# One block per layer for output projection, norm and feed-forward, and paged values loaded page by page

## The chip, the cores and the metric

The kernel runs on one core of one Trainium2 chip. A core has five engines that run their own instruction streams and meet through semaphores: TensorE (PE; its weight loads are listed as PEld), VectorE (DVE), ScalarE (ACT), GpSimd (POOL) and SyncE (SP, which here only issues DMAs). The metric is the device time of one execution in microseconds; less is better.

## The reference

One inference step of a two-layer decoder over T = 560 tokens: a prompt of 512 tokens behind 16 meta tokens, and 8 sequences with 4 new tokens each. Model width 1024, feed-forward width 2816, all in float32.

```python
for layer in range(2):
    xn = rmsnorm(h, norm_g[layer, 0])
    mix = mixer_even(...) if layer == 0 else mixer_odd(...)   # ends in "@ w_out"
    h = h + rmsnorm(mix, norm_g[layer, 1])
    ff = swiglu(rmsnorm(h, norm_g[layer, 2]), wg, wu, wd)     # (silu(x@wg) * (x@wu)) @ wd
    h = h + rmsnorm(ff, norm_g[layer, 3])
# in mixer_even, for the 8 sequences: attention over 1024 cached positions each
gather = lambda c: c[page_table].reshape((B, past) + c.shape[2:])     # 8 pages of 128 positions
hf = fox_attend(q, F, tq, concat(gather(cache_k), k), concat(gather(cache_v), v), F, tk)
```

## The kernel before

Activations lie with features on the 128 partitions and the 560 tokens along the columns, in two column halves of 280 (`HALF`), since a PSUM bank holds 512 floats. A matrix product keeps float32 accuracy by splitting each operand into a high part (rounded to the type fp32r) and a low part (the rest); three products per pair are summed: high*high, high*low, low*high. The weights come through `ring`, two slots in SBUF that SP fills by DMA. From a slot ScalarE makes `w_high` by a cast (L241) and VectorE `w_low` by a subtraction (L245), for one tile of 128 output features at a time, and TensorE works on the other of two such pieces meanwhile. One tile with 1024 inputs is 48 matmuls of 280 columns (8 input chunks, 3 products, 2 halves).

`project` is this loop as a block of its own: four semaphores tell when a piece is split, a tile finished and a bank free. `close_layer` ends a layer. In its first block it splits the mixer's output `xn` into `mixed_high` (ScalarE, L1779) and `mixed_low` (VectorE and GpSimd, L1786) and the first weights. Then follow three calls of `project` and one of `norm`: the output projection (8 tiles), the norms, gate and up (44 tiles in 11 turns of 4), down (8 tiles of 22 input chunks, each in two pieces of 66 matmuls). In gate and up, VectorE scales the gate by the norm's factor, ScalarE takes its silu, VectorE multiplies by up, and GpSimd scales again and splits the result into `hidden_high` and `hidden_low`.

`norm` squares the projection's output, sums the squares over the partitions by matmuls with a matrix of ones (L504), takes the root on ScalarE, and then walks over the 8 chunks at full width (560 columns): VectorE scales (L584) and adds to `h` (L588), ScalarE makes the next input's high part and its squares (L540, L541), VectorE the low part (L592, after all 8 chunks). TensorE sums the second squares; `warm` gives it idle matmuls in between. The root of the second norm is taken at the start of the next `project`, where VectorE then inverts it (L408). Every `with nc.Block()` ends in a barrier of all engines.

Attention over the cache (the block from L1530 on) takes the 8 sequences in two groups of 4. Step s of 16 works on one key page of each sequence of a group: `turned` transposes four pages on TensorE, `scores` follows one step behind. SP loads keys into two sets of four slots (`load_k`: four page numbers are read into registers, then four DMAs of 256 KB) and values into four buffers of eight pages (`load_v`: eight page numbers, eight DMAs). Three of the four value buffers of the first group are filled in the block before; the second group's can be filled only when `values(0)` (step 11) has used the first group's:

```python
load_v(sp, 2)
for s in range(2, STEPS):            # STEPS = 16
    load_k(sp, s)
    if s >= STEPS - 4:
        if s == STEPS - 4:
            sp.wait_ge(v_used, 1)
        load_v(sp, 4 + s - (STEPS - 4))
```

One of the value buffers lies in `ring`, so layer 0's output weights are sent only in the first block of `close_layer`; layer 1's are already there.

## Time and profile before

| | |
|---|---|
| median of 3 runs | 1977.45 us (1973.34 to 1980.96) |
| the profiled execution's own time | 1978.11 us |
| its span, first to last instruction | 1976.6 us |
| mean granted TensorE clock | 0.921 |
| TensorE busy | 1748.8 us (88%) |
| VectorE busy | 826.0 us (42%) |
| ScalarE busy | 488.9 us (25%) |
| GpSimd busy | 297.2 us (15%) |

The profile is of one execution; the times of a row are microseconds from the start of its span. A granted clock of 1.00 is TensorE at 2.4 GHz, 0.50 is 1.2 GHz. "Idle before" in a row is the time in which the engine had nothing to do ahead of the instruction, and behind the arrow stands what ended it; PEq is TensorE's sequencer, which as a releaser here stands for a barrier at the start or end of a block.

### The profile page before, as it was taken

Reading aid. Unit: us, or ns where it says so; the run is one execution under the profiler, and the core shown is the slowest. Engines: PE = TensorE matmul, PEld = TensorE weight load, DVE = VectorE, ACT = ScalarE, POOL = GpSimd, SP = SyncE. Lnnn points to the kernel's source line nnn. Section 1 sums busy time; section 2 is a strip of 40 time slices with the busy share of each in tenths; the row PEclk is TensorE's granted clock in tenths of the full one; section 3 lists DMA queues with packets and bytes.
Section 4 is the critical chain, followed back from the end, with each engine's and each line's share of the span. In section 5 each row is a group of like instructions: output and inputs, shape, how many; then the busy total and the mean of one; then the engine's idle time right before and its main releaser. Section 6 shows DMA issues by size and latency. Waiting matters only on the chain. (4 is left out here: it accounts for less than half of the span.)

```text
span 1976.6 us, 31237 instructions
## 1 busy us (share of the span) xinstructions
PE 1748.8 (88%) x12539; PEld 1577.6 (80%) x12539; DVE 826.0 (42%) x1427; ACT 488.9 (25%) x634; POOL 297.2 (15%) x290
## 2 busy tenths in 40 slices
PE   5999897696758899999899899978488999998995
PEld 5999854555438699999899699955286999998995
DVE  3323645524333744444222633267637444442225
ACT  3111310141111433332111311133214333321111
POOL 1411001001000033333200000031300333332000
PEclk9999987597879999999899999988689999999998
DMA  4232210155652133333222122220121333332321
GB/s 124 90 91 70 65 26 0 48 171 170 219 185 77 33 85 85 85 85 93 77 79 70 42 68 85 96 68 0 50 65 43 84 85 84 85 88 73 82 56 45
DMA packets 225241, 159.60 MB, mean 81 GB/s; under 512 B 18041, under 2 KB 206437, under 8 KB 225048
## 3 DMA queue, kind: packets, MB, share of 16 engines
q1 hardware_dynamic: 220832, 156.40, 27.1%
q0 software_dynamic: 3280, 1.85, 0.4%
q8 instruction: 38, 0.62, 0.1%
q10 hardware_dynamic: 1064, 0.51, 0.1%
q14 instruction: 27, 0.22, 0.0%
HBM read 149.11 MB, written 9.88 MB: 80 GB/s over the span
## 5 line engine op out<-in xcount | busy, mean ns | idle before, releaser
L241 ACT CAST w_high<-ring 128x1024 fp32r<-128x1024 f32 (+1 forms) x188 | 207.1, 1104 | 914.1 <-PE psum L334 911.4
L334 PE MATMUL psum<-mixed_high,w_high 128*128 128x280 f32 x1664 | 352.0, 293 | 35.3 <-PEq L1770 29.0
L245 DVE TENSOR_TENSOR w_low<-ring,w_high 128x1024 fp32r<-128x1024 f32 (+1 forms) x188 | 289.6, 1544 | 155.7 <-ACT w_high L241 153.4
L334 PE MATMUL psum<-mixed_high,w_low 128*128 128x280 f32 x1664 | 353.9, 294 | 0.0
L334 PE MATMUL psum<-mixed_low,w_high 128*128 128x280 f32 x1664 | 350.9, 293 | 0.0
L334 PEld LDWEIGHTS psum<-mixed_high,w_high 128*128 128x128 f32 x1664 | 267.4, 190 | 36.9 <-issue 36.9
L334 PEld LDWEIGHTS psum<-mixed_high,w_low 128*128 128x128 f32 x1664 | 267.9, 191 | 0.0
L334 PEld LDWEIGHTS psum<-mixed_low,w_high 128*128 128x128 f32 x1664 | 265.3, 190 | 0.0
L334 PE MATMUL psum<-normed_high,w_high 128*128 128x280 f32 x832 | 175.3, 292 | 3.8 <-PEq L517 3.8
L334 PE MATMUL psum<-normed_high,w_low 128*128 128x280 f32 x832 | 175.7, 292 | 0.0
L334 PE MATMUL psum<-normed_low,w_high 128*128 128x280 f32 x832 | 174.7, 292 | 0.0
L334 PE MATMUL psum<-hidden_high,w_high 128*128 128x280 f32 x704 | 149.3, 294 | 15.7 <-PEq L298 15.7
L334 PE MATMUL psum<-hidden_low,w_high 128*128 128x280 f32 x704 | 149.5, 294 | 0.0
L334 PE MATMUL psum<-hidden_high,w_low 128*128 128x280 f32 x704 | 149.2, 294 | 0.0
L334 PEld LDWEIGHTS psum<-normed_high,w_high 128*128 128x128 f32 x832 | 132.7, 189 | 4.7 <-issue 4.7
L334 PEld LDWEIGHTS psum<-normed_high,w_low 128*128 128x128 f32 x832 | 133.1, 190 | 0.0
L334 PEld LDWEIGHTS psum<-normed_low,w_high 128*128 128x128 f32 x832 | 132.0, 189 | 0.0
L334 PEld LDWEIGHTS psum<-hidden_high,w_high 128*128 128x128 f32 x704 | 113.0, 191 | 16.1 <-issue 16.1
L432 POOL TENSOR_TENSOR silu<-silu,rstd 128x560 f32<-128x560 f32 x44 | 63.6, 1446 | 409.4 <-DVE silu L385 409.4
L395 DVE TENSOR_TENSOR projected<-psum,rstd 128x280 f32 (+1 forms) x104 | 41.9, 444 | 194.3 <-PE psum L334 194.2
L334 PEld LDWEIGHTS psum<-hidden_high,w_low 128*128 128x128 f32 x704 | 112.9, 191 | 0.0
L334 PEld LDWEIGHTS psum<-hidden_low,w_high 128*128 128x128 f32 x704 | 112.5, 190 | 0.0
(350 smaller groups left out, 1983.7 us busy)
## 6 DMA issues: line engine op xcount, KB each, us to landing
ring<-in_ffn_wg SPq DMA_DIRECT2D x44, 512.0 KB, 4.0
ring<-in_ffn_wu SPq DMA_DIRECT2D x44, 512.0 KB, 5.2
ring<-in_ffn_wd SPq DMA_DIRECT2D x16, 1408.0 KB, 6.9
projected<-in_cache_fox_k SPq DMA_DIRECT2D x64, 256.0 KB, 4.1
ring<-in_w_in_even SPq DMA_DIRECT2D x14, 1024.0 KB, 5.5
ring<-in_w_in_odd SPq DMA_DIRECT2D x12, 1024.0 KB, 5.1
v_pages<-in_cache_fox_v SPq DMA_DIRECT2D x32, 256.0 KB, 4.3
projected<-in_cache_fox_v SPq DMA_DIRECT2D x16, 256.0 KB, 4.0
```

Of the source, the lines that this page charges most:

```text
L241: nc.scalar.copy(part(high, p), raw(slot, p)).then_inc(high_done[p], 1)
L245: nc.vector.tensor_tensor(part(low, p), raw(slot, p), part(high, p).bitcast(F32), ALU.subtract).then_inc(low_done[p], 1)
L334: last = nc.tensor.matmul(banks[2 * tl + half][:, 0:HALF], w[:, k, :], m[:, half * HALF:(half + 1) * HALF], start=(kk == 0 and w is w_high ...
L395: c = nc.vector.tensor_tensor(out, banks[2 * tl + half][:, 0:HALF], rstd[:, cols_], ALU.mult)
L432: nc.gpsimd.tensor_tensor(silu[:, slot, :], silu[:, slot, :], rstd[:, :], ALU.mult)
```

## The change

`close_layer` becomes one block. The first two units of gate and up weights (four tiles) get SBUF of their own (`first_w`) and are loaded and split during the output projection. The projection's tiles 0 to 5 run at full width, tiles 6 and 7 by halves: first both tiles for tokens 0 to 279, then both for tokens 280 to 559. The norms run for the first half of the tokens and then for the second; the squares are summed chunk by chunk on VectorE (`square_sum`, `h_square_sum`) and TensorE only sums the result over the partitions. As each chunk of a half comes out of the norm, TensorE multiplies it with the four first tiles (`first_products`). Gate and up go on with 10 turns, down follows without a barrier, its first piece waiting for 10 of the 11 turns of the hidden values and its second for all. The warming matmuls of this norm are gone. `hidden` is kept by halves, so GpSimd splits by halves. VectorE makes all of `mixed_low`.

For the cache, value buffer 2 of the first group is loaded two pages ahead of each of the key steps 2 to 5, and the second group's values by page number, one page of four sequences at a time (`load_v_step`), alternating with key steps 13 to 15, the rest behind them. `values(1)` waits for each page by itself.

The semaphores of three stages (the prompt's attention, the cache's, and each `close_layer`) are cleared and given back, with a barrier behind.

```diff
+    def stage_semaphores():
+        used = []
+        def new(name):
+            sems[name] = sems.get(name, 0) + 1
+            used.append(nc.alloc_semaphore(name=f"{name}_{sems[name]}"))
+            return used[-1]
+        def close():
+            nc.clear_and_free_semaphores(used)
+            nc.all_engine_barrier()
+        return new, close
...
+    def load_v_step(sp, pg):
+        _, pages = nc.values_load_multi_w_load_instructions(
+            step_ids[0:1, bass.ds(4 * (PAGES + pg), 4)], engines=[mybir.EngineType.SP], min_val=0, max_val=NPHYS - 1)
+        for slot, page in enumerate(pages):
+            sp.dma_start(vpage[slot][:, pg * 512:(pg + 1) * 512],
+                         cache_v[bass.ds(page, 1), :, :].rearrange("a t n -> (a t) n")).then_inc(v_step[pg], 16)
...
-            load_v(sp, 2)
             for s in range(2, STEPS):
+                if s < 6:
+                    load_v(sp, 2, 2 * (s - 2), 2)
                 load_k(sp, s)
-                if s >= STEPS - 4:
-                    if s == STEPS - 4:
-                        sp.wait_ge(v_used, 1)
-                    load_v(sp, 4 + s - (STEPS - 4))
+                if s == STEPS - 3:
+                    sp.wait_ge(v_used, 1)
+                if s >= STEPS - 3:
+                    load_v_step(sp, s - (STEPS - 3))
+            for pg in range(3, PAGES):
+                load_v_step(sp, pg)
...
+                for n in (6, 7):
+                    pe.wait_ge(w_lo[n % 2], 4)
+                    half_tile(n, 0).then_inc(half_done, 1)
+                pe.wait_ge(o_acc, 5)
+                mm(banks[1][:, 0:HALF], ones[:, :], acc[:, HALVES[0]], start=True, stop=False)
+                pe.wait_ge(o_sq, 13)
+                mm(banks[1][:, 0:HALF], ones[:, :], sq[6][:, HALVES[0]], start=False, stop=False)
+                half_tile(6, 1).then_inc(used[0], 1)
+                pe.wait_ge(o_sq, 14)
+                mm(banks[1][:, 0:HALF], ones[:, :], sq[7][:, HALVES[0]], start=False, stop=True).then_inc(o_sum, 1)
+                half_tile(7, 1).then_inc(used[1], 1)
...
+                def first_products(k, a, tiles):
+                    pe.wait_ge(xh_done, KC * a + k + 1)
+                    for t in tiles:
+                        bank = banks[2 * t + a][:, 0:HALF]
+                        if k == 0 and a == 0:
+                            pe.wait_ge(first_lo, t + 1)
+                        mm(bank, fw[t][0][:, k], x_h[:, k, HALVES[a]], start=(k == 0), stop=False)
+                        mm(bank, fw[t][1][:, k], x_h[:, k, HALVES[a]], start=False, stop=False)
+                    pe.wait_ge(xl_done, KC * a + k + 1)
+                    for t in tiles:
+                        last = mm(banks[2 * t + a][:, 0:HALF], fw[t][0][:, k], x_l[:, k, HALVES[a]], start=False,
+                                  stop=(k == KC - 1))
...
+                pe.wait_ge(h_acc, 2 * KC - 2)
+                pe.wait_ge(h_root, 1)
+                mm(banks[7][:, 0:HALF], ones[:, :], acc_h[:, HALVES[1]], start=True, stop=True).then_inc(h_sum, 1)
+                pe.wait_ge(h_root, 2)
+                for k in range(KC):
+                    first_products(k, 1, (3,))
...
+                            for s in range(2):
+                                pe.wait_ge(hid_done[s], 10 + p)
...
+                for a in range(2):
+                    c = HALVES[a]
+                    dve.wait_ge(o_root, a + 1)
+                    v.reciprocal(rpost[:, c], rpost[:, c])
...
+                    for step in range(KC + 3):
+                        k = step
+                        if k < KC:
+                            v.scalar_tensor_tensor(out=o[:, k, c], in0=o[:, k, c], scalar=gain(layer, 1, k), in1=rpost[:, c],
+                                                   op0=ALU.mult, op1=ALU.mult).then_inc(y_done, 1)
+                        k = step - 1
+                        if 0 <= k < KC:
+                            dve.wait_ge(y_done, KC * a + k + 1)
+                            v.tensor_tensor(h[:, k, c], h[:, k, c], o[:, k, c], ALU.add).then_inc(h_done, 1)
+                        k = step - 2
+                        if 0 <= k < KC:
+                            dve.wait_ge(xh_done, KC * a + k + 1)
+                            v.scalar_tensor_tensor(out=x_l[:, k, c], in0=h[:, k, c], scalar=gain(layer, 2, k),
+                                                   in1=x_h[:, k, c].bitcast(F32), op0=ALU.mult,
+                                                   op1=ALU.subtract).then_inc(xl_done, 1)
+                        k = step - 3
+                        if 1 <= k < KC:
+                            dve.wait_ge(h_sq, KC * a + k + 1)
...
+                            v.tensor_tensor(acc_h[:, c], sq[0][:, c] if k == 1 else acc_h[:, c], sq[k][:, c],
+                                            ALU.add).then_inc(h_acc, 1)
...
+                up_low(0, 0, 5)
+                for a in range(2):
+                    dve.wait_ge(h_root, a + 1)
+                    v.reciprocal(rstd[:, HALVES[a]], rstd[:, HALVES[a]])
```

Three places show the new order. On SP, at the start of the cache block, before (L1287 are values, L1281 keys; an ISA row prepares a register):

```order
L1287 ISA
L1287 DMA v_pages<-in_cache_fox_v 128x512
L1287 ISA
L1287 DMA v_pages<-in_cache_fox_v 128x512
L1275 TENSOR_LOAD step_ids
L1275 ISA x8
L1281 ISA
L1281 DMA projected<-in_cache_fox_k 128x512
L1281 ISA
L1281 DMA projected<-in_cache_fox_k 128x512
```

and SP at the same place now (L1305 are values, L1297 keys):

```order
L1302 TENSOR_LOAD page_ids
L1302 ISA x4
L1305 ISA
L1305 DMA v_pages<-in_cache_fox_v 128x512
L1305 ISA
L1305 DMA v_pages<-in_cache_fox_v 128x512
L1291 TENSOR_LOAD step_ids
L1291 ISA x8
L1297 ISA
L1297 DMA projected<-in_cache_fox_k 128x512
```

Two value pages now stand ahead of the first keys of this block; before there were eight, of which the rows show the last two.

On PE, between output projection and gate and up of a layer, before (L298, L543, L517 and L312 are branches into and out of blocks):

```order
L334 MATMUL psum<-mixed_high,w_low 128x280 x2
L316 REGISTER_ALU
L316 COMPARE_AND_BRANCH
L298 UNCONDITIONAL_BRANCH
L543 UNCONDITIONAL_BRANCH
L451 MATMUL psum<-ones 128x512 x4
L504 MATMUL psum<-squares,ones 128x280 x8
L451 MATMUL psum<-ones 128x512 x8
L504 MATMUL psum<-squares,ones 128x280 x16
L517 UNCONDITIONAL_BRANCH
```

and PE there now (L1889 ends the last half tile of the projection, L1937 to L1941 are `first_products`):

```order
L1889 MATMUL psum<-mixed_high_6555,w_low_6554 128x280
L1937 MATMUL psum<-mixed_high_6555,first_w_high_6561 128x280
L1938 MATMUL psum<-mixed_high_6555,first_w_low_6562 128x280
L1937 MATMUL psum<-mixed_high_6555,first_w_high_6561 128x280
L1938 MATMUL psum<-mixed_high_6555,first_w_low_6562 128x280
L1937 MATMUL psum<-mixed_high_6555,first_w_high_6561 128x280
L1938 MATMUL psum<-mixed_high_6555,first_w_low_6562 128x280
L1937 MATMUL psum<-mixed_high_6555,first_w_high_6561 128x280
L1938 MATMUL psum<-mixed_high_6555,first_w_low_6562 128x280
L1941 MATMUL psum<-mixed_low_6556,first_w_high_6561 128x280 x4
```

The sums and warming matmuls between the two products are gone from this place, and the second product starts chunk by chunk.

On DVE, in the norm, before (two rows of the scaling and adding loop, then all low parts):

```order
L584 SCALAR_TENSOR_TENSOR squares<-projected_out,cols,rstd 128x560
L588 TENSOR_TENSOR h<-h,squares 128x560 x2
L592 SCALAR_TENSOR_TENSOR mixed_low<-h,cols,mixed_high 128x560 x8
L517 UNCONDITIONAL_BRANCH
L369 UNCONDITIONAL_BRANCH
L408 RECIPROCAL rstd<-rstd 128x280 x2
```

and DVE in the norm now, one step of the first half:

```order
L2142 SCALAR_TENSOR_TENSOR projected_out_6548<-projected_out_6548,cols,post_rstd_6559 128x280
L2147 TENSOR_TENSOR h<-h,projected_out_6548 128x280
L2151 SCALAR_TENSOR_TENSOR mixed_low_6556<-h,cols,mixed_high_6555 128x280
L2159 TENSOR_TENSOR h_square_sum_6572<-squares_6563,squares_6564 128x280
```

The low part of a chunk now comes in the same step as its neighbours' scaling, at half the width, and a sum of squares has come to VectorE.

## Rows read from the trace of the kernel before

**Rows 1.** Windows: busy us by engine in stretches (us from the span's start)

```profile
core 0: us, PE busy (x) PEld busy (x) DVE busy (x) ACT busy (x) POOL busy (x), PEclk, DMA share, GB/s
525.00:563.00 38.00, 19.36 (x188) 16.25 (x190) 9.82 (x19) 4.68 (x8) 0.00 (x0) 0.65 0.83 271
649.30:679.80 30.50, 24.30 (x73) 12.91 (x73) 29.34 (x36) 17.53 (x27) 2.69 (x2) 1.00 0.00 1
706.00:953.20 247.20, 247.19 (x1923) 246.97 (x1921) 100.74 (x119) 77.71 (x78) 83.02 (x60) 1.00 0.33 88
953.20:961.00 7.80, 0.00 (x0) 0.00 (x0) 5.04 (x4) 1.36 (x1) 5.81 (x3) 0.70 0.00 1
961.00:966.60 5.60, 5.57 (x24) 5.57 (x25) 0.00 (x0) 0.00 (x0) 0.00 (x0) 0.50 0.88 243
```

**Rows 2.** Timeline, VectorE, norm of layer 0: start, us, line, operation

```profile
636.92 0.81 DVE L398 COPY projected_out<-psum 128x280 f32<-128x280 f32 x2 [3.81 <-PE psum L334]
649.27 0.81 DVE L398 COPY projected_out<-psum 128x280 f32<-128x280 f32 x2 [5.37 <-PE psum L334]
656.37 2.35 DVE L245 TENSOR_TENSOR w_low<-ring,w_high 128x1024 fp32r<-128x1024 f32 x2
663.87 0.73 DVE L588 TENSOR_TENSOR h<-h,squares 128x560 f32<-128x560 f32 x1
664.52 0.79 DVE L584 SCALAR_TENSOR_TENSOR squares<-projected_out,cols,rstd 128x560 f32<-128x560 f32 x1
673.36 5.78 DVE L592 SCALAR_TENSOR_TENSOR mixed_low<-h,cols,mixed_high 128x560 fp32r<-128x560 f32 x8
679.95 3.66 DVE L408 RECIPROCAL rstd<-rstd 128x280 f32<-128x280 f32 x2 [0.81 <-ACT rstd L357]
```

**Rows 3.** Timeline, ScalarE, layer 0, behind the projection and behind the fourth up tile

```profile
650.37 2.35 ACT L525 ACTIVATE squares<-projected_out 128x560 f32<-128x560 f32 x4 [12.41 <-PEq L298]
679.42 0.88 ACT L357 ACTIVATE rstd<-psum,eps 128x280 f32<-128x280 f32 x2 [4.06 <-PEq L517]
706.30 1.05 ACT L241 CAST w_high<-ring 128x1024 fp32r<-128x1024 f32 x1 [4.50 <-PE psum L334]
```

**Rows 4.** Timeline, VectorE, an operation of 280 columns in the odd layer

```profile
1412.96 1.31 DVE L2130 SCALAR_TENSOR_TENSOR mixed<-mixed,cols,psum 128x280 f32<-128x280 f32 x3
```

**Rows 5.** Timeline, GpSimd, last hidden tile of layer 0

```profile
958.99 1.36 POOL L437 TENSOR_TENSOR hidden_low<-silu,hidden_high 128x560 f32 x1 [0.21 <-issue]
```

**Rows 6.** Timelines, start of `close_layer` in both layers

```profile
591.67 1.04 ACT L241 CAST w_high<-ring 128x1024 fp32r<-128x1024 f32 x1 [2.15 <-DMA ring<-in_w_out_even]
598.14 0.83 PE L334 MATMUL psum<-mixed_high,w_high 128*128 128x280 f32 x2 [13.88 <-PEq L1770]
1428.92 3.46 ACT L1779 CAST mixed_high<-mixed 128x560 fp32r<-128x560 f32 x6 [4.04 <-PEq L461]
1439.41 0.83 PE L334 MATMUL psum<-mixed_high,w_high 128*128 128x280 f32 x2 [15.13 <-PEq L1770]
```

**Rows 7.** Waits of TensorE over the span: us in total, times, longest

```profile
PE psum L1563 <- DMA projected<-in_cache_fox_k: 23.8, 6, 9.6
```

**Rows 8.** Timeline, SP's DMA queue in the cache block

```profile
527.56 4.29 SPq L1287 DMA_DIRECT2D projected<-in_cache_fox_v  x8
533.41 1.89 SPq L1281 DMA_DIRECT2D projected<-in_cache_fox_k  x4
554.23 1.88 SPq L1281 DMA_DIRECT2D projected<-in_cache_fox_k  x4
558.89 4.02 SPq L1287 DMA_DIRECT2D ring<-in_cache_fox_v  x8
```

**Rows 9.** Timelines, VectorE, first and last of the cache's output

```profile
524.84 0.75 DVE L1700 TENSOR_SCALAR past_probs<-psum,fst 128x512 f32<-128x512 f32 x1 [8.70 <-PE psum L1614]
582.80 0.75 DVE L1700 TENSOR_SCALAR past_probs<-psum,fst 128x512 f32<-128x512 f32 x1 [10.91 <-PE psum L1614]
```

**Rows 10.** Page, part 6: DMA issues, KB each, us to landing

```profile
v_pages<-in_cache_fox_v SPq DMA_DIRECT2D x32, 256.0 KB, 4.3
```

More of the change, by code:

```diff
@@ new lines, in _ @@
+                for u in (2, 3):
+                    when_split(u - 1)
+                    send(sp, units[0], u % 2, u)
+                for u in (2, 3):
+                    when_split(u + 1)
+                    send(sp, up[layer], u % 2, u)
+                with sp.Fori(0, 9) as i:
+                    for slot in range(2):
+                        when_split(i * 2 + (5 + slot))
+                        send(sp, up[layer], slot, i * 2 + (4 + slot))
+                with sp.Fori(0, 4) as i:
+                    for slot in range(2):
+                        when_split(i * 2 + (23 + slot))
+                        send(sp, down[layer], slot, i * 2 + slot)
@@ L1804, in close_layer @@
-        project(units[0], 1, 2, KC, chunk(x), o, 0, pieces, then=up[layer], split=True)
-        norm(o, (layer, 1), (layer, 2), squares, x, splitters(2, KC, pieces, True))
-        inner_.close()
-        inner_ = ExitStack()
-        hid = put_split(inner_, "hidden", FC, "left")
-        silu = ExitStack()
-        project(up[layer], 2, FC // 2, KC, chunk(x), hid, 0, pieces, then=down[layer],
-                silu=place(silu, "silu", [128, 2, T]), normed=True, following=(1, FC, False))
-        silu.close()
@@ L1813, in close_layer @@
[L1813 to L1816 removed]
+                g = nc.gpsimd
+                with pool.Fori(0, 11) as i:
+                    for slot in range(2):
+                        pool.wait_ge(tile_evac[2 * slot + 1], i + 1)
+                        g.tensor_tensor(silu[:, slot, :], silu[:, slot, :], rstd[:, :], ALU.mult)
+                        g.drain()
+                        hh, hl = ([t[:, bass.ds(i * 2 + slot, 1), :].rearrange("p a t -> p (a t)") for t in a]
+                                  for a in (hid_h, hid_l))
+                        for a in range(2):
+                            g.tensor_copy(hh[a], silu[:, slot, HALVES[a]])
+                        g.drain()
+                        for a in range(2):
+                            last = g.tensor_tensor(hl[a], silu[:, slot, HALVES[a]], hh[a].bitcast(F32), ALU.subtract)
+                        last.then_inc(hid_done[slot], 1)
@@ L1818, in hybrid_decoder @@
+        close_sems()
+        ffn_out = out
     close_layer(0, (out_even, odd), True)
```

362 lines of the change are left out of this document (319 added, 43 removed).

## The prediction

> **What bounds the kernel now.** I read the page first (TensorE busy 88% of the span), then TensorE's waits, then windows over the stages, then timelines around each place where TensorE stands still. In gate and up TensorE is busy 247.19 of 247.20 us at a granted clock of 1.00 [rows 1]: 1923 matmuls, 0.1285 us each, so a tile of 48 takes 6.17 us. There only less TensorE work would help, and the change leaves that loop as it is. The time that can be won lies between the loops. In the norm of a layer, 30.5 us from 649.3, TensorE shows 24.3 us busy, but with 73 warming and summing matmuls, while VectorE is busy 29.3 [rows 1]: VectorE is the bound there. Between up and down TensorE stands for 7.8 us, and the next 5.6 us run at 0.50, 1.2 GHz, half of its 2.4 [rows 1]. At the start of `close_layer` it waits 13.9 and 15.1 us [rows 6]. In the cache block it waits 23.8 us for keys [rows 7], and from 525 to 563 it is busy half the time while the DMA engines are busy 83% [rows 1].
>
> **The norm, twice.** Count from the end of the projection's sixth tile, when VectorE copies it at 636.92 [rows 2]. Before, the fourth up tile ended at 706.30 [rows 3], 69.4 us later. In the changed kernel the chain from the same point is:
> - two half tiles and one more, 72 matmuls of 0.1285 us, 9.3 us; three sums, at about 0.3 each (24.3 us over 73 records, [rows 1]), 0.9. Together 10.2.
> - ScalarE's root, half of 0.88 [rows 3], and the inversion of one half, half of 3.66 [rows 2]: 2.3. The other half tile hides under them. Now 12.5.
> - VectorE's steps, 8 chunks in each half: 32 operations of the scaling kind and 30 additions, all of 280 columns. For scaling [rows 4] show 1.31 us for three, 0.44. Additions of 280 from SBUF are in no row; at full width they start 0.65 us apart (663.87 to 664.52), and the scaling kind 0.72 (5.78 for eight) [rows 2], which at half width becomes 0.44, so 0.28 less; I take 0.37. That is 14.1 + 11.1 = 25.2, plus the second half's inversion 1.8, plus two starts that wait for ScalarE's first chunk, about 0.6 each: 28.2. Now 40.7. The 192 first products (24.7 us) run under this chain, save the last 24 (3.1), which stand beside the next item.
> - VectorE's low part of the next weights (half of 2.35), two inversions (3.66) and the scaling of the first tile (0.81) [rows 2]: 5.6. The fifth up tile can start at 46.3.
>
> That gives 69.4 - 46.3 = 23.1 us a layer. TensorE's own work would allow 27: 288 matmuls (37.0) and eight sums (2.4), with the root and inversion where it idles (2.3). The other bound has operations of half width as long as full ones: 32 x 0.72 + 30 x 0.65 = 42.5 instead of 25.2, 17 us more, a gain of 6. I take 21, near the row of 280 columns, two off for the handshakes between VectorE and ScalarE in every step. Two layers: 42.
>
> A rule speaks against halves. The Trainium skill, page "VectorE: DVE Perf Modes", section on the TRN2 errata, says that SBUF operations pay a fixed extra time each and should have 512 elements or more. By its formula, (N + 151) cycles at 0.96 GHz, an addition takes 0.45 us at 280 columns, and the 62 operations 27.8 us instead of 25.2, 5 us more in two layers. The trace agrees on the length at 560 (0.73 by [rows 2], 0.74 by the formula) but shows the next start after 0.65.
>
> **Up to down, twice.** The barrier goes. Down's first piece waits for 10 turns of hidden values, long done; GpSimd ends the last one at 960.35 [rows 5], 7.2 us after TensorE's last up matmul. The first piece covers it: 66 matmuls, 8.5 us. If that cover fails, the excess alone is lost. Gained: 7.8, and half of the 5.6 at the low clock, 2.8: 10.6 a layer, 21 in two; bounds 15 (the clock is not won) and 21.
>
> **The start of `close_layer`.** In layer 0 ScalarE casts the weights when they land, at 591.67 [rows 6]; then come one chunk's high part (0.6), the low weights (1.2, beside it) and one low chunk (0.7), so TensorE starts at about 594.8 instead of 598.14 [rows 6]: 3.3. VectorE then makes a low chunk in 0.72 and TensorE uses one in 0.77, so that it does not starve. In layer 1 the weights are there: 1428.92 plus 1.05, 1.2 and 1.0 is 1432.2 instead of 1439.41 [rows 6], 7.2. Together 10.5; bounds 4 and 12. The 2 MB of first weights are queued behind the projection's first 2 MB and have two tiles, 12.3 us, to land; at 243 GB/s [rows 1] they need 8.6.
>
> **The cache block.** `values(0)` ends at 524.84 [rows 9], and only then may SP send the second values. Its own pace is one four-page unit per 3.45 us (from 531.85, the end of one row, to 535.30, the end of the next) [rows 8]. Before, the last keys went out behind 8 + 4 + 8 + 4 + 8 pages, at 556.11 [rows 8], and the output came at 582.80 [rows 9], 26.7 later. Now they are the fourth unit, 13.8 us behind 524.84: 538.6, 17.5 earlier, output at 565.3. The other chain is the eighth value page, the tenth unit: sent at 559.3, landed 4.3 later [rows 10] at 563.6, and with its own products, some 2 us, 565.6. The ten units are 10.5 MB; at the 271 GB/s of that window [rows 1] they take 38.7 us, to 563.5, so the transfers allow it just so. The keys of step 2 stand behind two pages instead of eight, but steps 3 to 5 then carry six pages each; I count nothing for it. Gain 17, bounds 11 (landing behind a full queue, products at the low clock) and 21.
>
> **The clearing of semaphores**, four times, each with a barrier. A barrier takes 0.3 us (650.08 to 650.37) [rows 2, 3]; the clearing by GpSimd is in no row, from nothing to the 1.36 of a GpSimd operation [rows 5]. I take 0.5 each, -2; bounds -1 and -7. GpSimd's splitting in halves and VectorE's larger share of `mixed_low` lie under TensorE's tiles.
>
> **Sum.** 42 + 21 + 10.5 + 17 - 2 = 88.5 us off the profiled execution's 1978.1 gives 1889.6; the median of the runs is 0.7 below that execution, so **1889**.
>
> **Rivals.**
> - *Half-width operations cost nearly what full ones do* (the bound above): 34 us of the norm's gain gone, about 1924. For it: no row has an addition of 280 columns from SBUF. Against: [rows 4].
> - *The values gain nothing* because the DMA engines, 83% busy in their window, bring them as late as before: 1906. Against: SP reads numbers between the loads, and TensorE there waits for keys, which now stand further ahead.
> - *The first weights don't hide*, and ScalarE, which takes its work in order, waits for them ahead of the projection's next piece: 8.6 us a layer, 1906. The change would still do what it says.
> - *Slower: TensorE loses its clock.* In the second half it has 9 matmuls a chunk, 1.16 us, where VectorE needs 1.62, so it stands 28% of the time. If the clock falls there and stays at 1.2 GHz in the up loop, every microsecond of that loop costs another. With 44 us of a layer's 247 at the low clock the whole gain is gone; with all of it the time is some 1889 + 494 = 2383. For it: the clock is 0.65 where TensorE is busy 19.4 of 38 us. Against: after the 7.8 us stall steady work had it back to 1.00 within 5.6 us [rows 1]. The Trainium skill, "TensorE: Matmul & The Clock Gate", section on HAM oscillation, warns that waits between short bursts take the clock again and again; that bears on the half itself, where at the low clock a chunk takes 2.1 us instead of 1.62, some 4 us a layer, not on the loop behind it.
>
> **How the numbers follow.** The forecast with its bounds, 0.70; costly half operations 0.12; no gain from the values 0.07; unhidden first weights 0.05; loss of the clock with a slower kernel 0.03; several terms falling flat at once, to within half a per cent, 0.03. The range reaches from 1870 (norm 25 a layer, cache 21, start 12) to 1922, which takes in the late values and weights and most of the costly halves. About half a per cent, 10 us, is what a measurement of this kernel can tell from no change; faster by more 0.94, within it 0.03, slower 0.03.
>
> **What would show it.** In the profile after: no long stand of TensorE between up and down; first products within 2 us of the projection's last half tile; VectorE busy without gaps through both halves, its additions of 280 columns near 0.37 apart; the fifth up tile 46 to 49 us behind the sixth projection tile; SP's last value page near 559 (less what came earlier) and the output of the cache 15 to 19 us earlier. Wrong would be: additions near 0.6, TensorE waiting for `x_low` at 0.50, a wait for `first_w`, or up tiles longer than 6.2 us.

## The result and the profile after

The changed kernel takes 1894.38 us (median of 4 runs, 1891.92 to 1898.12), beside 1978.55 for the kernel before on the same chip; the ratio is 0.958 with a 95% interval of 0.9554 to 0.9605, 84 us less. The forecast was 1889. The profiled execution takes 1898.12 us, 80.0 less than that of the kernel before, and the account below is made of these two.

Windows of the changed kernel: the second half of the cache block, the first matmuls of `close_layer`, the first and the second half of the norm, the start of down, and the norm behind down.

```profile
core 0: us, PE busy (x) PEld busy (x) DVE busy (x) ACT busy (x) POOL busy (x), PEclk, DMA share, GB/s
530.50:569.00 38.50, 29.40 (x320) 18.16 (x323) 12.73 (x26) 5.35 (x9) 0.00 (x0) 0.78 0.84 274
583.90:588.40 4.50, 4.50 (x19) 4.50 (x20) 4.50 (x7) 3.36 (x6) 0.00 (x0) 0.50 1.21 290
634.00:652.40 18.40, 17.02 (x126) 16.30 (x124) 16.09 (x33) 8.78 (x22) 0.00 (x0) 1.00 0.01 1
652.40:669.80 17.40, 14.52 (x101) 13.25 (x100) 17.15 (x35) 10.52 (x21) 0.00 (x0) 1.00 0.00 0
918.00:923.60 5.60, 5.60 (x46) 5.60 (x45) 3.14 (x3) 1.35 (x1) 4.31 (x5) 1.00 0.07 20
1054.90:1061.30 6.40, 5.24 (x9) 2.25 (x10) 5.18 (x6) 5.24 (x7) 2.69 (x2) 0.73 0.01 1
```

In the norm's two halves VectorE is busy 16.1 of 18.4 and 17.2 of 17.4 us, as in [rows 1], but beside it TensorE is now at work for 17.0 and 14.5 us at a granted clock of 1.00, nearly all of it products that are needed anyway (in the first window also the end of the projection's last half tile, to 637.0). At down's start TensorE is busy all the time at 1.00, where it stood for 7.8 us and then ran at 0.50. The low clock is still there at the start of the projection (0.50), behind down (0.73) and in parts of the cache block (0.78, before 0.65).

The timeline of VectorE in layer 0 (start, us, line, operation): the copy of the sixth projection tile, steps of the norm with the last one at 664.06, and the scaling of the fifth up tile:

```profile
623.32 0.81 DVE L2116 COPY projected_out<-psum 128x280 f32<-128x280 f32 x2 [1.53 <-PE psum L1883]
...
637.33 0.44 DVE L2147 TENSOR_TENSOR h<-h,projected_out 128x280 f32<-128x280 f32 x1
637.69 0.50 DVE L2142 SCALAR_TENSOR_TENSOR projected_out<-projected_out,cols,post_rstd 128x280 f32<-128x280 f32 x1
...
644.15 0.51 DVE L2151 SCALAR_TENSOR_TENSOR mixed_low<-h,cols,mixed_high 128x280 fp32r<-128x280 f32 x1 [1.63 <-ACT mixed_high L2043]
...
664.06 1.00 DVE L2159 TENSOR_TENSOR h_square_sum<-h_square_sum,squares 128x280 f32<-128x280 f32 x2
...
677.22 0.80 DVE L2174 TENSOR_TENSOR silu<-rstd,psum 128x280 f32<-128x280 f32 x2 [2.41 <-PE psum L1883]
```

The operation behind an addition of 280 columns starts after 0.36 us (637.33 to 637.69), which no row of the kernel before could show. One wait stands within VectorE's steps, 1.63 us at 644.15.

TensorE at the same place: the first product of each half, and the fifth up tile.

```profile
638.39 0.40 PE L1937 MATMUL psum<-mixed_high,first_w_high 128*128 128x280 f32 x1 [1.38 <-ACT mixed_high L2043]
...
654.42 0.40 PE L1937 MATMUL psum<-mixed_high,first_w_high 128*128 128x280 f32 x1 [2.01 <-ACT mixed_high L2043]
...
670.79 0.50 PE L1883 MATMUL psum<-mixed_high,w_high 128*128 128x280 f32 x2 [0.98 <-DVE silu L2174]
```

The first product comes 1.4 us behind the last half tile. TensorE then stands still for 2.0 us between the halves, where VectorE's inversion and first steps come ahead of the next chunk, and for 1.0 at the end.

The starts of `close_layer` (ScalarE's first cast and TensorE's first matmul in layer 0, TensorE's in layer 1), and GpSimd's last hidden tile of layer 0:

```profile
580.79 1.04 ACT L1994 CAST w_high<-ring 128x1024 fp32r<-128x1024 f32 x1 [24.39 <-DMA ring<-in_w_out_even]
583.90 0.81 PE L1883 MATMUL psum<-mixed_high,w_high 128*128 128x280 f32 x2 [10.95 <-DVE mixed_low L2109]
1388.54 0.80 PE L1883 MATMUL psum<-mixed_high,w_high 128*128 128x280 f32 x2 [7.77 <-DVE mixed_low L2109]
923.33 0.78 POOL L2232 TENSOR_TENSOR hidden_low_b<-silu,hidden_high_b 128x280 f32 x1
```

These answer to [rows 5, 6]: TensorE starts 3.1 us behind the cast in layer 0, where it was 6.5 (3.4 less), and its wait in layer 1 falls from 15.13 to 7.77 (7.4 less). GpSimd ends at 924.1, 6.1 us behind the last up tile (918.0), under down's first piece.

The cache block: VectorE's first and last output, SP's queue from the first to the last second value, and TensorE's waits for keys over the span.

```profile
528.76 0.75 DVE L1733 TENSOR_SCALAR past_probs<-psum,fst 128x512 f32<-128x512 f32 x1 [8.82 <-PE psum L1647]
571.02 0.75 DVE L1733 TENSOR_SCALAR past_probs<-psum,fst 128x512 f32<-128x512 f32 x1 [12.11 <-PE psum L1647]
```

```profile
530.57 0.34 SPq L1312 DMA_DIRECT2D projected<-in_cache_fox_v  x1
...
534.02 2.54 SPq L1297 DMA_DIRECT2D projected<-in_cache_fox_k  x4
...
564.04 0.33 SPq L1312 DMA_DIRECT2D ring<-in_cache_fox_v  x1
```

```profile
PE psum L1593 <- DMA projected<-in_cache_fox_k: 9.6, 7, 3.0
```

The waits for keys fall from 23.8 us [rows 7] to 9.6, and the output comes at 571.02 instead of 582.80 [rows 9].

Behind down, the norm's first squares and its inversion on VectorE and the first warming matmuls on TensorE, of the kernel before and then of the changed kernel:

```profile
1100.72 3.27 DVE L567 TENSOR_TENSOR squares<-ffn_out 128x560 f32<-128x560 f32 x2 [0.33 <-PEq L298]
...
1109.00 3.67 DVE L580 RECIPROCAL rstd<-rstd 128x280 f32<-128x280 f32 x2
1100.71 3.67 PE L451 MATMUL psum<-ones 128*128 128x512 f32 x8 [1.16 <-PEq L298]
```

```profile
1056.07 3.27 DVE L581 TENSOR_TENSOR squares<-ffn_out 128x560 f32<-128x560 f32 x2 [1.14 <-PEq L128]
...
1065.29 3.67 DVE L594 RECIPROCAL rstd<-rstd 128x280 f32<-128x280 f32 x2 [0.91 <-ACT rstd L547]
1056.06 5.37 PE L465 MATMUL psum<-ones 128*128 128x512 f32 x8 [1.97 <-PEq L128]
```

The norm starts 1.14 us behind down's last copy and not 0.33: the clearing with its barrier. Then its warming matmuls run at the low clock (5.37 us for eight, before 3.67), the sums come later, and the inversion starts 9.22 instead of 8.28 us behind the first squares.

The account of the 80.0 us, each stage by the same two events in both traces (the fourth row by TensorE's wait):

| stage | before | after | gained | forecast |
|---|---|---|---|---|
| span's start to TensorE's first cached key | 462.11 | 463.51 | -1.4 | -0.5 (clearing) |
| first key to the cache's output | 120.69 | 107.51 | 13.2 | 17 |
| output to the first matmul of `close_layer`, layer 0 | 15.34 | 12.88 | 2.5 | 2.8 (3.3 - 0.5) |
| layer 1, TensorE's wait there | 15.13 | 7.77 | 7.4 | 7.2 |
| first matmul to the copy of the sixth tile, both layers | 78.40 | 79.27 | -0.9 | 0 |
| sixth to fifth up tile, both layers | 151.27 | 107.80 | 43.5 | 42 |
| last up tile to the last copy of down, both layers | 291.6 | 272.3 | 19.4 | 21 |
| last copy of down to the norm's inversion, both | 18.82 | 22.24 | -3.4 | -1 |

The stages sum to 80.1, and the rest of the span gives 0.1 back. Of the -1.4 in the first row 0.9 stands in the trace before the first clearing, so that the clearing itself took 0.5 there. Each row is the difference of one execution of each kernel, and that of the changed kernel is the slowest of its four, 3.7 us above their median.

### The profile page after: what moved, and what is told of

Its sections match the earlier page's. It is cut to its first block and busy times, and to the rows that moved or that the text cites. A ratio compares the mean times of both kernels' runs of the same rounds, so it can differ in the third digit from the quotient of the medians.

```text
span 1896.6 us, 31249 instructions
## 1 busy us (share of the span) xinstructions
PE 1711.6 (90%) x12427; PEld 1553.7 (82%) x12427; DVE 829.7 (44%) x1503; ACT 450.5 (24%) x656; POOL 292.4 (15%) x368
## 5 line engine op out<-in xcount | busy, mean ns | idle before, releaser
L1883 PE MATMUL psum<-mixed_high,w_high 128*128 128x280 f32 x1472 | 310.5, 292 | 20.7 <-DVE mixed_low L2109 18.7
L1883 PE MATMUL psum<-mixed_high,w_low 128*128 128x280 f32 x1472 | 312.4, 294 | 0.0
L1883 PE MATMUL psum<-mixed_low,w_high 128*128 128x280 f32 x1472 | 309.6, 292 | 0.0
L1994 ACT CAST w_high<-ring 128x1024 fp32r<-128x1024 f32 (+1 forms) x128 | 144.5, 1129 | 659.1 <-PE psum L1883 630.7
L2101 DVE TENSOR_TENSOR w_low<-ring,w_high 128x1024 fp32r<-128x1024 f32 (+1 forms) x128 | 212.7, 1662 | 141.8 <-ACT w_high L1994 141.8
L255 ACT CAST w_high<-ring 128x1024 fp32r<-128x1024 f32 x52 | 54.4, 1050 | 254.0 <-PE psum L348 253.3
L2174 DVE TENSOR_TENSOR silu<-silu,psum 128x280 f32<-128x280 f32 x88 | 35.3, 442 | 155.9 <-PE psum L1883 154.3
L1883 PE MATMUL psum<-hidden_low_b,w_high 128*128 128x280 f32 x352 | 102.8, 292 | 0.0
L1883 PE MATMUL psum<-hidden_high_b,w_high 128*128 128x280 f32 x352 | 102.8, 292 | 0.0
L1883 PE MATMUL psum<-hidden_high_a,w_high 128*128 128x280 f32 x352 | 102.6, 292 | 0.0
L1883 PE MATMUL psum<-hidden_high_b,w_low 128*128 128x280 f32 x352 | 102.4, 291 | 0.0
```

The lines of the kernel that those rows point to most:

```text
L255: nc.scalar.copy(part(high, p), raw(slot, p)).then_inc(high_done[p], 1)
L1883: done = mm(banks[2 * tl + a][:, 0:HALF], w, m[a], start=first and s == 0, stop=last and s == 2)
L1994: nc.scalar.copy(dst, src).then_inc(w_hi[p], 1)
L2101: v.tensor_tensor(dst, src, high_.bitcast(F32), ALU.subtract).then_inc(w_lo[p], 1)
L2174: last = v.tensor_tensor(silu[:, slot, c], silu[:, slot, c] if p else rstd[:, c], banks[2 * q + a][:, 0:HALF], ALU.mult)
```

## Experiments

Each kernel ran with the kernel before on the same chip (medians of 1975.8 to 1978.7). A time stands beside its ratio to that kernel, with the interval; the changed kernel's is 0.958.

**The old value loading in the changed kernel** (e1).

```diff
-            for s in range(2, STEPS):
-                if s < 6:
-                    load_v(sp, 2, 2 * (s - 2), 2)
-                load_k(sp, s)
-                if s == STEPS - 3:
-                    sp.wait_ge(v_used, 1)
-                if s >= STEPS - 3:
-                    load_v_step(sp, s - (STEPS - 3))
-            for pg in range(3, PAGES):
-                load_v_step(sp, pg)
+            load_v(sp, 2)
+            for s in range(2, STEPS):
+                load_k(sp, s)
+                if s >= STEPS - 4:
+                    if s == STEPS - 4:
+                        sp.wait_ge(v_used, 1)
+                    load_v(sp, 4 + s - (STEPS - 4))
```

> The changed kernel with the value loading of the kernel before (buffer 2 whole ahead of the keys, the second group's values buffer by buffer). In the changed kernel the cache's output stands at 571.02 instead of 582.80 and the block starts 0.87 later, so the value loading should be worth 12.6 us. If that is so, the output comes at 583.7 and the time is 1894 + 12.6 = 1907. If the output came earlier for another reason (the keys or the block's start), it stays near 571 and the time near 1895.

Measured: 1908.19 (0.9644, 0.963 to 0.9659), 13.8 us slower. VectorE's first and last output of the cache:

```profile
531.19 0.75 DVE L1727 TENSOR_SCALAR past_probs<-psum,fst 128x512 f32<-128x512 f32 x1 [14.05 <-PE psum L1641]
586.71 0.75 DVE L1727 TENSOR_SCALAR past_probs<-psum,fst 128x512 f32<-128x512 f32 x1 [8.19 <-PE psum L1641]
```

From one to the other it is 55.5 us, beside 42.3 in the changed kernel and 58.0 before. So the earlier output comes from the value loading, and the time agrees with the 13 us that the account gives it; by the two intervals it could be some 7 to 18.

**First products only when the norm is done** (e2). TensorE makes all sums first, then all products.

```diff
-                for k in range(KC):
-                    first_products(k, 0, range(4))
...
-                for k in range(KC):
-                    first_products(k, 1, range(3))
...
                 pe.wait_ge(h_root, 2)
-                for k in range(KC):
-                    first_products(k, 1, (3,))
+                for a in range(2):
+                    for k in range(KC):
+                        first_products(k, a, range(4))
```

> TensorE makes the first products of gate and up only when both halves of the norm are done; VectorE's chain is as it was. If the norm's gain is the overlap of these products with VectorE's steps, the 192 products (24.7 us, some 2 more at the low clock) stand behind the root of the second half at 666 instead of the 24 that stand there now: the fifth up tile starts near 693 instead of 670.8, 22 us later in each layer, time 1894 + 45 = 1939. If the gain came from VectorE's chain itself (halves, sums moved, no barriers), the time rises by less than 10.

Measured: 1939.6 (0.9802, 0.9787 to 0.9817), 45.2 us slower. VectorE's first scaling of a gate tile:

```profile
691.00 0.80 DVE L2169 TENSOR_TENSOR silu<-rstd,psum 128x280 f32<-128x280 f32 x2 [24.27 <-PE psum L1941]
```

VectorE now waits 24.27 us for the products. From the sixth to the fifth up tile it is 76.2 us in either layer, beside 53.9 in the changed kernel and 75.6 before: all that the two norms gained is gone. What was won there is that the second product runs under VectorE's chain, and not that the chain became shorter.

**Down's first piece waits for all hidden values** (e3).

```diff
-                                pe.wait_ge(hid_done[s], 10 + p)
+                                pe.wait_ge(hid_done[s], 11)
```

> Down's first piece waits for all 11 turns of hidden values instead of 10. If the gain between up and down comes from covering GpSimd's last turn with the first piece, TensorE stands still from 918.0 to the end of GpSimd's last operation at 924.1, 6.1 us, and then loses half of some 5 us at the low clock: 8.5 us a layer, time 1894 + 17 = 1911. If it came from the barrier and the branches themselves, the wait costs under 2 us a layer and the time stays under 1899.

Measured: 1910.32 (0.9666, 0.965 to 0.9682), 15.9 us slower. TensorE's first matmul of down and the window behind it:

```profile
922.65 0.57 PE L1883 MATMUL psum<-hidden_high_a,w_high 128*128 128x280 f32 x1 [6.26 <-POOL hidden_low_b L2232]
```

```profile
922.60:928.50 5.90, 5.85 (x28) 5.88 (x29) 0.00 (x0) 0.00 (x0) 0.00 (x0) 0.58 0.73 194
```

It waits 6.26 us for GpSimd's last part, and the next 5.9 run at a mean clock of 0.58. From the last up tile to the last copy of down the two layers take 16.9 us more than in the changed kernel, of the 19.4 that were gained. So most of the gain between up and down is the cover by the first piece, with the clock; 2.4 us are left for the barrier and the branches, which no run takes apart.

**Value buffer 2 whole, as before** (e4).

```diff
+            load_v(sp, 2)
             for s in range(2, STEPS):
-                if s < 6:
-                    load_v(sp, 2, 2 * (s - 2), 2)
                 load_k(sp, s)
```

> Value buffer 2 loaded whole ahead of the keys as before; the second group's values still page by page. If values(0) ends 3 us later in the changed kernel (528.76 against 524.84, of which 0.87 is the later start) because SP reads page numbers four times instead of once, 1.5 us each, it now ends at 525.7, and the time is 1894 - 3 = 1891. If the full DMA engines set that place (264 to 282 GB/s in both kernels), values(0) stays within 1 us of 528.8 and the time within 1. If the keys of steps 2 to 5 that come earlier are worth something, the time rises.

Measured: 1895.61 (0.9578, 0.956 to 0.9595), no difference. Its outputs:

```profile
527.03 0.75 DVE L1732 TENSOR_SCALAR past_probs<-psum,fst 128x512 f32<-128x512 f32 x1 [9.63 <-PE psum L1646]
570.84 0.75 DVE L1732 TENSOR_SCALAR past_probs<-psum,fst 128x512 f32<-128x512 f32 x1 [14.20 <-PE psum L1646]
```

The first came 1.7 us earlier and the second did not. Counted from the first cached key, the first output stands at 60.7 to 65.3 in the kernels that have the changed loading of this buffer, and at 63.6 here, 66.8 in e1 and 62.7 before, which load it whole. The 2.5 us that the changed kernel's first output comes later than before lie within this scatter, and the theory that the three added reads cost them finds no support.

**Page numbers read ahead** (e5).

```diff
                 if s == STEPS - 3:
+                    for pg in range(4):
+                        v_step_numbers(pg)
                     sp.wait_ge(v_used, 1)
...
     def load_v_step(sp, pg):
-        _, pages = nc.values_load_multi_w_load_instructions(...)
-        for slot, page in enumerate(pages):
+        if pg not in v_numbers:
+            v_step_numbers(pg)
+        for slot, page in enumerate(v_numbers[pg]):
```

> SP reads the page numbers of the first four units of second values before it waits for values(0), where it stands idle from 521.2 to 528.8, and not behind it: 1.45 us less for each of four units. If SP's pace (3.45 us a unit) sets the end of the cache block, the last value page goes out 5.8 us earlier and the time is 1894 - 5.8 = 1888.5. If the DMA engines set it (10.5 MB at 271 GB/s are 38.7 us from the first send), the pages wait in the queue instead, the output stays 42 to 45 us behind values(0), and the time stays within 1.5 of 1894.

Measured: 1888.6 (0.9549, 0.9535 to 0.9562), 5.8 us faster than the changed kernel; all five runs lie below its lowest. Outputs, and SP's first and last second value:

```profile
523.97 0.75 DVE L1741 TENSOR_SCALAR past_probs<-psum,fst 128x512 f32<-128x512 f32 x1 [8.71 <-PE psum L1655]
560.60 0.75 DVE L1741 TENSOR_SCALAR past_probs<-psum,fst 128x512 f32<-128x512 f32 x1 [9.88 <-PE psum L1655]
```

```profile
524.10 0.34 SPq L1318 DMA_DIRECT2D projected<-in_cache_fox_v  x1
...
554.16 0.33 SPq L1318 DMA_DIRECT2D ring<-in_cache_fox_v  x1
```

The first value goes out 0.1 us behind values(0) instead of 1.8, the last 30.2 behind instead of 35.3, and the output 36.6 behind instead of 42.3. So SP's pace set the end of the cache block, and the transfers follow it.

**Clearing later** (e6): GpSimd clears the semaphores inside the next block (`clear_now`), and the barrier of the clearing goes.

```diff
-            nc.clear_and_free_semaphores(used)
-            nc.all_engine_barrier()
+            to_clear.append(used)
...
+                clear_now()
```

> The four clearings of semaphores are done by GpSimd inside the next block, without a barrier of their own. From the trace of the changed kernel a clearing with its barrier takes 0.87 us, and behind down it also lets TensorE's clock fall, so that the next norm's sums end 0.9 later: 2 x 0.87 + 2 x 1.8 = 5.3, time 1889. If the clock there falls in any case, only 4 x 0.87 = 3.5 come back, 1891. If they cost the 0.5 each of the forecast, 2 come back, 1892.4.

Measured: 1890.89 (0.9558, 0.9544 to 0.9572), 3.5 us less than the changed kernel by the medians; the two intervals overlap, so that the time alone does not show a gain. Behind down:

```profile
1051.30 3.27 DVE L591 TENSOR_TENSOR squares<-ffn_out 128x560 f32<-128x560 f32 x2 [0.34 <-PEq L1853]
...
1059.57 3.67 DVE L604 RECIPROCAL rstd<-rstd 128x280 f32<-128x280 f32 x2
1051.28 3.67 PE L474 MATMUL psum<-ones 128*128 128x512 f32 x8 [1.17 <-PEq L1853]
```

The norm starts 0.34 us behind the copy, the eight warming matmuls take 3.67 again, and the inversion comes 8.27 behind the squares, and 9.42 behind the copy in both layers, instead of 11.17 and 11.07. But with the clearing the clock does not fall every time. The same place of layer 0 in e2, which keeps the clearing:

```profile
1076.17 3.67 PE L465 MATMUL psum<-ones 128*128 128x512 f32 x8 [1.97 <-PEq L128]
```

The same 1.97 us without a matmul, and the eight keep the high clock. Over the profiles of all kernels the place stands 18 times with the clearing (1.78 to 1.97 us without a matmul), and the clock fell in 9 of them, in the changed kernel both times; it stands 10 times without (1.16 us), and the clock fell in none. So a clearing behind down costs 0.6 to 0.8 us each time and, in half of the cases seen, some 0.9 more through the clock. How much the two clearings ahead of the layers take is left open within the scatter.

**Sums of the second half on TensorE** (e7), where VectorE adds squares in the first half only, and **the same with the late clearing** (e8).

```diff
-                        if 1 <= k < KC:
+                        if a == 0 and 1 <= k < KC:
...
+                    if k >= 4:
+                        for j in range(k) if k == 4 else (k - 1,):
+                            pe.wait_ge(h_sq, KC + j + 1)
+                            mm(banks[7][:, 0:HALF], ones[:, :], sq[j][:, HALVES[1]], start=(j == 0), stop=False)
```

> In the second half the squares of h are summed by eight matmuls of TensorE and no longer by seven additions of VectorE (0.36 us each). If VectorE alone sets the second half, it ends 2.5 us earlier in each layer, time 1894 - 5 = 1889. If TensorE or the handshake with ScalarE sets it as much, the added matmuls (0.9 us) take the gain back, and the time stays within 1.5 of 1894.

> Both edits before this one together: if their gains are independent, 1894 - 5.3 - 5 = 1884.

Measured: 1898.65 (0.9594, 0.9575 to 0.9612), and together with the late clearing 1893.19 (0.9582, 0.9558 to 0.9606). Neither can be told from the changed kernel, and the gains expected, to 1889 and 1884, did not come. In both profiles the sixth to the fifth up tile takes 55.7 us a layer instead of 53.9. TensorE's last two sums and VectorE's inversion of the second half:

```profile
668.17 0.64 PE L1964 MATMUL psum<-squares,ones 128*128 128x280 f32 x2
668.64 0.64 PE L1966 MATMUL psum<-squares,ones 128*128 128x280 f32 x2
669.84 1.91 DVE L2196 RECIPROCAL rstd<-rstd 128x280 f32<-128x280 f32 x1 [2.61 <-ACT rstd L2042]
```

A sum takes two records and 0.47 us (668.17 to 668.64), not the 0.1285 of a product that the expectation reckoned with: eight are 3.8 us, more than the 2.9 that TensorE stood still in that half, 2.0 of them ahead of its first product. VectorE ended its steps earlier and then waited 2.61 us for the root. In the changed kernel the second half is bound by VectorE, but TensorE is close behind and takes over with these sums.

**Sums of the second half on GpSimd** (e9), the same additions in its program ahead of the hidden values.

```diff
-                        if 1 <= k < KC:
+                        if a == 0 and 1 <= k < KC:
...
+                for k in range(1, KC):
+                    pool.wait_ge(h_sq, KC + k + 1)
+                    pool.wait_ge(h_acc, KC - 1 + k - 1)
+                    g.tensor_tensor(acc_h[:, HALVES[1]], sq[0][:, HALVES[1]] if k == 1 else acc_h[:, HALVES[1]],
+                                    sq[k][:, HALVES[1]], ALU.add).then_inc(h_acc, 1)
```

> In the second half GpSimd, which stands idle there, adds the squares of h and VectorE doesn't (seven additions of 280 columns; GpSimd takes 0.79 for one, VectorE 0.36). If VectorE sets the second half and the two engines don't hinder each other, it ends 2.5 us earlier in each layer, time 1894 - 5 = 1889. If GpSimd's work holds VectorE up, as where a subtraction of VectorE takes 2.35 instead of 1.23 us beside a GpSimd operation of 1.39 (684.48 in the changed kernel's trace), VectorE loses some 0.8 us for each us of GpSimd's 5.3, 4 in place of the 2.5 saved, and the time is 1894 + 3 = 1897. If TensorE sets the second half, the time stays within 1.5 of 1894.

Measured: 1895.85 (0.958, 0.9567 to 0.9594), no gain, and 55.1 us a layer from the sixth to the fifth up tile instead of 53.9. GpSimd's first addition, VectorE's operation beside it, and the same operation between two of GpSimd's additions:

```profile
658.58 0.89 POOL L2224 TENSOR_TENSOR h_square_sum<-squares,squares 128x280 f32<-128x280 f32 x1 [149.16 <-ACT squares L2044]
658.72 1.05 DVE L2151 SCALAR_TENSOR_TENSOR mixed_low<-h,cols,mixed_high 128x280 fp32r<-128x280 f32 x1
...
661.06 0.50 DVE L2151 SCALAR_TENSOR_TENSOR mixed_low<-h,cols,mixed_high 128x280 fp32r<-128x280 f32 x1
```

VectorE's operation beside the addition takes 1.05 us instead of 0.50. What VectorE saves it loses again. The Trainium skill, "SBUF — State Buffer", section on the two separate sides, says that a GpSimd operation and a VectorE operation with two SBUF inputs lock the same port pair and the later one stands still for the whole instruction; the trace agrees, since VectorE's operation starts 0.14 us behind GpSimd's and ends 0.30 behind its end (659.77 to 659.47).

**All page numbers ahead, buffer 2's by one read, late clearing** (e10).

```diff
                 if s == STEPS - 3:
-                    for pg in range(4):
+                    for pg in range(8):
                         v_step_numbers(pg)
```

> The clearings as in the run before (3.5 us), and SP reads all page numbers of the second values ahead of the wait for values(0), with the time for it from one read of the numbers of buffer 2 instead of four. Against the run with four units read ahead, four more reads of 1.45 us leave the path. If SP's pace still sets the end, 1888.6 - 3.5 - 5.8 = 1879. If the DMA engines take over (10.5 MB in the 34 us that they had in that run, 309 GB/s, is then all they do), the reads bring nothing more, and the time is 1888.6 - 3.5 = 1885.

Measured: 1882.95 (0.951, 0.9496 to 0.9525). It lies between the two expectations. VectorE's first output and SP's first second value:

```profile
526.15 0.75 DVE L1755 TENSOR_SCALAR past_probs<-psum,fst 128x512 f32<-128x512 f32 x1 [8.79 <-PE psum L1669]
529.03 0.34 SPq L1328 DMA_DIRECT2D projected<-in_cache_fox_v  x1
```

Eight sets of numbers are more than the wait holds. SP still reads the last of them when values(0) is done, and the first value goes out 2.9 us behind it, beside 0.1 in e5. The last output stands 37.3 us behind the first, no nearer than the 36.6 of e5, although no wait of TensorE for a value page is left at the end. So the four added reads brought the cache block nothing in these profiles; whether fewer reads ahead than eight would gain more than four is not tested.

**TensorE starts with the whole input split** (e11).

```diff
-                        if n == 0:
-                            pe.wait_ge(mix_h, k + 1)
-                            pe.wait_ge(mix_l, k + 1)
+                        if n == 0 and k == 0:
+                            pe.wait_ge(mix_h, KC)
+                            pe.wait_ge(mix_l, KC)
```

> At the start of the projection TensorE waits for all eight chunks of the mixer's output to be split, not for the first alone. VectorE ends the eighth low part at 589.45 and 1394.1 in the changed kernel, where TensorE starts at 583.90 and 1388.54. If the start chunk by chunk is what gained 10 us, TensorE starts 5.5 us later in each layer, time 1894 + 11 = 1905. If VectorE's low parts pace the first tile anyway, so that TensorE only stood still later, the time stays within 3 of 1894.

Measured: 1904.2 (0.9632, 0.9612 to 0.9652), 9.8 us slower. TensorE's first matmul in layer 0:

```profile
588.79 0.81 PE L1883 MATMUL psum<-mixed_high,w_high 128*128 128x280 f32 x2 [16.32 <-DVE mixed_low L2109]
```

Its wait grows from 10.95 to 16.32, and in layer 1 from 7.77 to 13.46. The start chunk by chunk is worth about what the account shows (9.9 us).

**The second root later** (e12), on the kernel of e10.

```diff
-                        if a == 0 and k == 2:
+                        if a == 0 and k == 4:
                             act.wait_ge(o_sum, 2)
```

> The kernel of the run with all page numbers read ahead and late clearings, with ScalarE's root for the second half of the post norm taken behind chunk 4 instead of chunk 2. In the changed kernel ScalarE waits 2.55 us for TensorE's sum ahead of that root (643.20), with chunk 3's high part behind it, and VectorE then waits 1.63 for chunk 3. If VectorE's chain sets the first half, that wait goes and each layer is 1.6 us shorter: 1883 - 3.2 = 1879.8. If TensorE, with 12 products a chunk (1.54 us), sets the first half as much as VectorE (1.56), the wait moves to TensorE's products and the time stays within 1 of 1883.

Measured: 1878.25 (0.9509, 0.9485 to 0.9533). By its median it is the fastest of all, but the kernel before was 2.3 us faster in these runs too, and the ratio cannot be told from that of e10. In the traces the place itself is clear; copies of the sixth tile and the scaling of the fifth up tile, first of e10, then of e12:

```profile
614.53 0.81 DVE L2138 COPY projected_out<-psum 128x280 f32<-128x280 f32 x2 [1.53 <-PE psum L1905]
668.43 0.80 DVE L2196 TENSOR_TENSOR silu<-rstd,psum 128x280 f32<-128x280 f32 x2 [2.41 <-PE psum L1905]
```

```profile
613.00 0.81 DVE L2138 COPY projected_out<-psum 128x280 f32<-128x280 f32 x2 [1.53 <-PE psum L1905]
665.21 0.80 DVE L2196 TENSOR_TENSOR silu<-rstd,psum 128x280 f32<-128x280 f32 x2 [2.43 <-PE psum L1905]
```

53.90 and 52.21 us: 1.7 a layer, as VectorE's chain would have it.

## Why the prediction was right, and where it was off

The time lay in the range, 5 us above the forecast, and the mechanisms were those that the prediction named. Its steps, in its order:

- **The norm, 21 us a layer.** Measured 21.7. The chain came as it was built: root at 10.6 us behind the sixth tile (10.2 forecast; a sum takes 0.47, not 0.3), VectorE's first step at 13.2 (12.5), its last step at 41.7 (40.7), the fifth up tile at 47.5 (46.3). The disputed price, additions of 280 columns, is 0.36, beside 0.37 taken, so the rival of costly halves falls. The rule of the Trainium skill in "VectorE: DVE Perf Modes", section on the TRN2 errata, gives 0.45 us; the row's own length is 0.43 to 0.44 and agrees, but the next operation starts after 0.36, and the chain goes by that. That the gain needs the products under the chain is shown by e2. The two waits of 0.6 at the starts of the halves did not come; in their place stands the one of 1.6 at 644.15, because ScalarE waits 2.55 us for a sum ahead of a root with the next chunk's part behind it (e12).
- **Up to down, 10.6 us a layer.** Measured 10.2 and 9.1. TensorE does not stand, the clock stays at 1.00, and GpSimd's turn ends under the first piece; e3 takes 15.9 of it back by that wait alone.
- **The starts, 10.5.** From the cast in layer 0 and by the wait in layer 1 they gain 3.4 and 7.4; e11 shows that the chunks do it. What was not forecast: the first six tiles take 0.9 us longer in two layers, since in layer 0 the low clock lasts through the first 4.5 us (0.50 from 583.9 to 588.4, before 0.64 over the same stretch). It does not come every time: in e3, with the same start, the clock is 0.64 there and the six tiles take 38.8 us, as before.
- **The cache, 17.** This is the term that was mis-sized: the account has 13.2, and e1 has 13.8. The mechanism was right, SP's 3.45 us a unit, and e5 shows it. But from values(0) to the output it is 42.3 us and not 40.8: the last page is sent 35.6 behind values(0) (34.5 taken; one unit took 4.1), lands 4.5 later (4.3), and the end takes 2.1 (2). In the profiles of the other eight kernels with this loading of the second values it is 42.7 to 45.0, so the forecast took each step at its best. The other 2.5 us of this profile, a later values(0), lie within the scatter (e4).
- **The clearings, -2.** Too small: behind down they cost 3.4 in the account, over half of it (0.94 a layer) through TensorE's clock, which the forecast left out. That it fell in both layers was bad luck of this execution; where it doesn't fall, a clearing there costs 0.6 to 0.8 (e6), still more than the 0.5 taken. The bound was -7.
- **The first weights hide**, as forecast: ScalarE's cast of them stands at 600.31, behind TensorE's second tile, and waits for no transfer there. **TensorE keeps its clock** in the second half: 1.00 with TensorE busy 14.5 of 17.4 us, and the up loop keeps its pace (240.7 and 240.8 us from the fifth tile to the last), so the slower rival falls.

The profiled execution gained 80.0 where 88.5 was forecast. Of these 8.5 us the cache is 3.8, the clearings (first and last row of the account) 3.3, up to down 1.6 and the six tiles 0.9, against which the norm gave 1.5 more than taken. The median missed by 5 only, since that execution is the slowest of the four; how the 5 are shared out no run tells. The range's lower end, 1870, was not worked out: the three terms that the prediction names for it give 1889 - 8 - 4 - 1.5 = 1875.5. Nothing here hangs on it.

## What to carry to other kernels

Where one engine bounds a stage, look for work of another that can start from its results piece by piece: VectorE's norm is no shorter than before, and 21.7 us a layer were won since TensorE makes products from each chunk. When a queue's engine reads page numbers between transfers, those reads are part of the transfer's path; read them while the queue waits for a buffer, and no more of them than that wait holds (four sets gained here, eight outlasted it). A clearing with its barrier behind down cost 0.6 to 0.8 us here, and about twice that in the half of the cases in which TensorE's clock fell behind it.

## What the hardware showed beyond expectation

- The length of a stand of TensorE alone does not tell whether its clock falls. Behind down, 1.78 to 1.97 us without a matmul were followed by eight warming matmuls of 5.37 us in 9 places, at a mean clock of 0.73 in that window, and of 3.67 in 9 others. Between the norm's halves TensorE stood for 2.01 us or more in each layer of eleven kernels, and the granted clock stayed at 1.00 in all of them.
- A matmul that sums squares over the partitions holds TensorE 0.47 us for 280 columns, 3.7 times a product of the same width from fp32r operands (0.1285) (e7).
- GpSimd's addition of 280 columns lengthens a VectorE operation of the same width beside it from 0.50 to 1.05 us (e9).
